# A hybrid encoder step: queries and keys turned and split out of the projection

## The chip, the cores and the metric

One NeuronCore of a Trainium2 chip runs the whole step. The metric is the device time of one execution in microseconds (us). Before the change it is 2070.28 us, the median of three runs (2068.09 to 2095.45).

## The reference, cut to what matters

A layer runs over two groups of requests that share weights: a prompt of 1024 rows and 8 sequences of 16 new rows each with a past of 256 rows. All in F32, width 1024.

```
xn = rmsnorm(x, g_attn)
aq,ak,av, bq,bk,bv, cq,ck,cv, dq,dk,dv, df = split(xn @ w_in)      # w_in: 1024 x 2820
A, 4 heads of 64: stick-breaking:  w = exp(logsig(z) - sum of softplus(z) over later keys)
B, 4 heads of 64, 2 key heads: window of 128 keys, table bias, a sink in the softmax
C, 4 heads of 2 x 32: two softmax maps (q1 k1, q2 k2) with table bias,
                      (p1 - lam * p2) @ v, rmsnorm of the head's output
D, 4 heads of 64: softmax(q k / 8 + f_q - f_k) @ v, f a running sum of log gates
h = x + concat(A,B,C,D) @ w_out
h = h + relu(rmsnorm(h) @ w_up)^2 @ w_down
h = h + sigmoid(h @ w_ple_gate) * (p @ w_ple_proj);   y = rmsnorm(h)
```

Outputs are y, and for each group its new keys and values (for B's sample the rolled window) and log gates.

## The kernel before, in words

The 1152 rows (1024 of the prompt, 128 of the sample) are nine tiles of 128 rows. The kernel is a series of blocks (projection, attention, output projection, MLP, gate and final norm), each with a barrier at its end. Matrix products use F32R, a type in which a value is split into a high part (a cast on ScalarE, ACT) and a low part (a subtraction on VectorE, DVE); `three` (L104 to L107) sums high x high, high x low and low x high. The weights come through a ring of four raw slots on the sync queue (SP), `w_load`, `w_split_hi`, `w_split_lo` (L87 to L102).

**Projection** (L196 to L443). `w_in` is cut in 6 chunks of 470 columns. For each chunk and each of the nine row tiles, TensorE (PE) runs 8 x 3 matmuls with the rows' tile stationary and 470 columns moving into one of three PSUM banks, ACT copies the bank to `proj_out`, and GpSimd (POOL) stores it to the DRAM tensor `proj_rows` (1152 x 2820), rows as rows. ACT and DVE split the next chunk's weights meanwhile. In chunk 0 the rows are also normed and turned. In the last chunk PE makes the bias table's rows and the gates' sums.

**Attention** (L473 to L1257). The order is written out by hand. A loop of two turns (`heads_loop`) runs 8 heads each, A, A, B, B, C, C, D, D (`JOBS`, even and odd), each over nine tiles: tiles 0 to 7 are 128 queries of the prompt against all earlier keys (B: at most 256), tile 8 is the sample with 272 keys of each of its 8 sequences (B: 144). All engines go through steps s. In step s PE makes the scores of tile s + 1 (`scores`, L1160), turns the weights of tile s - 1 (`turn_tile`, L1200) and multiplies those of tile s - 2 with the values (`values`, L1215). The scores are in two PSUM areas `S`, used in turn; a C tile takes both, one a map, and in the kernel before a map waits only for its own area (L1174 to L1179). DVE's step: for A a sum, a scan and a difference (`stick_breaking`, L984), for the others the row maximum (`maximum`, L998), for C also the difference of the maps (`combine`, L1034), then the head's output (`out`, L1055). ACT has the exponentials and copies turned weights out of PSUM.

A head's queries and keys are loaded by SP as rows of 64 numbers (`k_rows`, `q_rows`, `k_cache_rows`, L726 to L728, packets of 256 B), as soon as the head before has been copied. Preparing the next head is spread over tiles 1 to 5 of the present one (`AFTER`, `prep_chunks`, L584 to L595), in 9 chunks (2 of keys, 2 of queries, one mixed of sample keys and queries, 4 of cached keys; B has 2 of these). A chunk is: DVE writes each row twice side by side (`twice`, L917), PE turns four 128x128 blocks (L1139), ACT takes the high part out of PSUM (L809 to L825) and DVE the low part (`prep`, L936 to L957). So queries lie with their high part in rows 0 to 63 of the partitions and their low part in 64 to 127 (C: 32 and 32 for each map), keys stand twice, once as high parts (`k_turned_hi`) and once as low parts (`k_turned_lo`). Two matmuls (L1194; L1187 for the sample, with the queries spread over blocks of zeros) then give all four products. Their width is at least 256 columns. Masks and biases are added by a matmul of the identity with the F32 mask (L1197).

The first head of a turn of the loop is prepared before its first scores (L1076 to L1082, L1244). Values, bias tables and gates come in a second group of transfers, L731 to L747, issued when all tiles of the head before the previous one are done. DVE adds masks to the bias or the gates for the next head in step 6 of the present one (`bias` and `sample_gates`, L959 to L982, called in L1112), after `job_loaded`. POOL copies keys and values from `proj_rows` to the outputs (L759).

## Time and profile before

| | us |
|---|---|
| median of three runs | 2070.28 |
| the profiled execution | 2087.65 |
| its span, first to last instruction | 2086.0 |
| PE busy in it | 1927.6 (92%) |
| DVE busy | 938.8 (45%) |
| ACT busy | 693.5 (33%) |
| mean granted clock of PE, of full | 0.933 |

The rows come from one execution, taken by the hardware profiler. PE is TensorE's matmuls, PEld its weight loads, which overlap them. An F32 matmul is listed as two records. A record of a matmul holds its whole latency, so the spacing of starts tells what one costs in a row of them. The granted clock is given as a share of full speed (2.4 GHz). L12 is line 12 of the kernel. "<-" names what ended an idle time.

### The profile page before, as it was taken

How to read it: one execution, taken by the hardware profiler on the slowest of the kernel's cores; microseconds unless marked ns; L12 is line 12 of the kernel's file. 1: busy time of each engine (PE TensorE's matmuls, PEld its weight loads, DVE VectorE, ACT ScalarE, POOL GpSimd, SP SyncE). 2: the span in 40 equal slices, each digit the busy share in tenths (PEclk: the TensorE clock that was granted, in tenths of full speed). 3: DMA queues.
4: the chain of work that ended last, by engine and by line, in shares of the span. 5: the costliest groups of instructions: out<-in, count | busy, mean ns of one | idle time of the engine just before them, and what ended most of it. 6: DMA issues, size and time to landing. Idle time of an engine off the chain costs nothing. (4 is left out here: it accounts for less than half of the span.)

```text
span 2086.0 us, 29729 instructions
## 1 busy us (share of the span) xinstructions
PE 1927.6 (92%) x10334; PEld 1694.7 (81%) x10334; DVE 938.8 (45%) x1826; ACT 693.5 (33%) x1474; POOL 88.9 (4%) x152
## 2 busy tenths in 40 slices
PE   7999994789998679999798999999999999999898
PEld 6888883677877577778687989899998989998686
DVE  4211125877375877767345333333333333333434
ACT  5211114654254655445223222222221212211326
POOL 0111100000000000000110000000000000000000
PEclk9999996898599779989899999999999999999999
DMA  5322324344122326222431111111111111110202
GB/s 176 104 91 88 85 74 79 77 113 79 29 58 57 54 70 136 48 58 61 163 111 46 41 41 41 44 49 53 49 49 43 41 41 41 41 41 20 86 28 94
DMA packets 189252, 140.94 MB, mean 68 GB/s; under 512 B 147588, under 2 KB 157508, under 8 KB 189096
## 3 DMA queue, kind: packets, MB, share of 16 engines
q1 hardware_dynamic: 160696, 99.73, 18.7%
q0 software_dynamic: 9728, 34.63, 4.8%
q10 hardware_dynamic: 18688, 4.72, 0.9%
q8 instruction: 88, 1.44, 0.3%
q14 instruction: 52, 0.43, 0.1%
HBM read 114.95 MB, written 32.35 MB: 71 GB/s over the span
## 5 line engine op out<-in xcount | busy, mean ns | idle before, releaser
L105 PE MATMUL up<-xt_hi,w_hi_even 128*128 128x384 f32 x768 | 258.1, 336 | 1.9 <-PEq L1285 1.9
L107 PE MATMUL up<-xt_hi,w_lo_even 128*128 128x384 f32 x768 | 257.7, 336 | 0.0
L106 PE MATMUL up<-xt_lo,w_hi_even 128*128 128x384 f32 x768 | 257.6, 335 | 0.0
L107 PE MATMUL down<-w_hi_odd_b,hidden_lo 128*128 128x512 f32 x576 | 224.5, 390 | 0.0
L106 PE MATMUL down<-w_lo_odd_b,hidden_hi 128*128 128x512 f32 x576 | 224.5, 390 | 0.0
L105 PE MATMUL down<-w_hi_odd_b,hidden_hi 128*128 128x512 f32 x576 | 224.0, 389 | 0.0
L1494 DVE TENSOR_TENSOR h_rows<-down,h_rows 128x1024 f32<-128x1024 f32 x72 | 88.2, 1225 | 235.3 <-PE down L107 235.3
L1459 ACT ACTIVATE hidden_rows<-up 128x384 f32<-128x384 f32 x96 | 47.3, 492 | 415.5 <-PE up L107 415.5
L1227 PE MATMUL outs<-v_rows,probs_turned 128*128 128x64 f32 x984 | 144.0, 295 | 14.2 <-DVE probs_turned L680 11.5
L1227 PEld LDWEIGHTS outs<-v_rows,probs_turned 128*128 128x128 f32 x984 | 138.5, 216 | 19.4 <-DVE head_out L1063 7.5
L1487 DVE TENSOR_TENSOR hidden_rows<-hidden_rows 128x384 f32<-128x384 f32 x96 | 53.6, 558 | 222.8 <-ACT hidden_rows L1459 222.8
L105 PEld LDWEIGHTS up<-xt_hi,w_hi_even 128*128 128x128 f32 x768 | 144.9, 189 | 3.6 <-DVE xt_lo L132 2.1
L106 PEld LDWEIGHTS up<-xt_lo,w_hi_even 128*128 128x128 f32 x768 | 145.0, 189 | 0.8
L107 PEld LDWEIGHTS up<-xt_hi,w_lo_even 128*128 128x128 f32 x768 | 144.8, 189 | 0.0
L1212 PE MATMUL turns<-cst,probs 128*128 128x128 f32 x520 | 97.2, 311 | 35.0 <-DVE probs_turned L680 22.7
L107 PEld LDWEIGHTS down<-w_hi_odd_b,hidden_lo 128*128 128x128 f32 x576 | 108.1, 188 | 22.5
L106 PEld LDWEIGHTS down<-w_lo_odd_b,hidden_hi 128*128 128x128 f32 x576 | 108.1, 188 | 22.0
L105 PEld LDWEIGHTS down<-w_hi_odd_b,hidden_hi 128*128 128x128 f32 x576 | 108.2, 188 | 21.9
L1139 PE MATMUL turns<-cst,rows_twice 128*128 128x128 f32 x512 | 93.3, 329 | 30.8 <-DVE rows_twice L930 23.4
L680 ACT COPY probs_turned<-turns 128x512 f32<-128x512 f32 (+3 forms) x156 | 69.0, 459 | 146.9 <-PE turns L1212 146.6
L1194 PE MATMUL scores<-k_turned_hi,q_turned 128*128 128x256 f32 (+4 forms) x224 | 100.5, 449 | 14.3 <-ACT probs L856 7.5
L1212 PEld LDWEIGHTS turns<-cst,probs 128*128 128x128 f32 x520 | 74.3, 163 | 46.4 <-DVE probs_turned L680 20.7
(232 smaller groups left out, 3673.8 us busy)
## 6 DMA issues: line engine op xcount, KB each, us to landing
w_raw<-w_up SPq DMA_DIRECT2D x64, 256.0 KB, 3.0
w_raw<-w_down SPq DMA_DIRECT2D x64, 256.0 KB, 3.4
proj_rows<-proj_out POOLq DMA_DIRECT2D x54, 235.0 KB, 2.4
w_raw<-w_in SPq DMA_DIRECT2D x48, 235.0 KB, 2.7
k_rows<-proj_rows SPq DMA_DIRECT2D x16, 288.0 KB, 3.3
q_rows<-proj_rows SPq DMA_DIRECT2D x16, 288.0 KB, 4.1
v_rows<-proj_rows SPq DMA_DIRECT2D x16, 288.0 KB, 3.4
head_rows<-head_out ACTq DMA_DIRECT2D x16, 288.0 KB, 3.1
```

What stands on the lines that cost most here:

```text
L105: nc.tensor.matmul(out, xh, wh, start=first, stop=False)
L106: nc.tensor.matmul(out, xh, wl, start=False, stop=False)
L107: return nc.tensor.matmul(out, xl, wh, start=False, stop=last)
L680: copy(pt[i % 2][:, b * P:b * P + k], TB[n % 3][:, 0:k]).then_inc(q[f"read{n % 3}"], 1)
L1139: last = nc.tensor.transpose(bank[:, y * P:(y + 1) * P], tw[:, PREP[chunk] % TW, y, :], ident)
L1194: nc.tensor.matmul(dst[:, c:c + w], qt[own, e, P * t:P * (t + 1)], kt[part][own, e, k0 + c:k0 + c + w], start=part == 0, stop=False, skip_ ...
L1212: last = nc.tensor.transpose(TB[n % 3][:, (y - b) * P:(y - b + 1) * P], block_src, ident)
L1227: last = nc.tensor.matmul(dst, w[:, y * P:(y + 1) * P], vr[:, e, first_block(i) + y, :], start=y == 0, stop=y == nb - 1)
L1459: nc.scalar.activation(R[:, f % 2, :], U[f][:, 0:GT], ACT.Relu).then_inc(relu_d, 1)
L1487: nc.vector.tensor_tensor(R[:, f % 2, :], R[:, f % 2, :], R[:, f % 2, :], ALU.mult).then_inc(sq_d, 1)
L1494: nc.vector.tensor_tensor(H[:, t, :], DN[t % 2][:, :], H[:, t, :], ALU.add).then_inc(dn_add, 1)
```

## The change

It moves the turning and splitting out of attention into the projection, and changes how scores are made.

- `w_in` is taken in six blocks: 388 columns (values of A and B, gates), then the queries and keys of A, B, C and D, then 512 columns (values of C and D). Value blocks work as before and are stored as `value_rows` (1152 x 896). Queries and keys come out turned: for each of 15 pieces of 128 columns (two heads) and each group of three row tiles the weights are stationary and 384 rows moving (45 units). ACT scales queries and takes the high part, DVE the low part, POOL stores both (`q_turned_*`, `k_turned_*`).
- New keys are also kept in F32 (`kf`) and turned back by PE for the key outputs (19 turns, 56 transposes); cached keys are loaded by SP, turned for two heads at a time by PE, split by ACT and DVE, and stored (`k_cache_turned_*`, 26 turns of four transposes). PE does a turn right behind a unit's matmuls, with the two banks `TP`.
- In attention, all chunks are gone with their waits. SP loads each head in one group, at the point where values were loaded: keys, queries straight, queries crossed (low part where the high one was), cached keys, new sample keys and both kinds of spread sample queries (packets of 64 B), values, bias, gates. PE waits for the whole group before a head's first scores.
- Keys lie once, high and low part in the two halves; the second matmul uses the crossed queries. The widths are no longer raised to 256 columns.
- The two maps of a C head alternate, matmul by matmul; both wait for both score areas.
- Masks and the identity are rounded to F32R, a bias is split in two F32R parts (two more DVE instructions a head), so masks take one F32R matmul and biases two. The sample's additions stay F32.

```diff
-CW = D_IN // CHUNKS
+GT = 3 * P
+NG = TILES // 3
...
+            BLOCKS = ((388, ((512, 256), (1152, 128), (DF_COL, 4))), (512, ((0, 512),)), (384, ((768, 384),)),
+                      (512, ((1280, 512),)), (512, ((2048, 512),)), (512, ((1792, 256), (2560, 256))))
+            PIECES = {"A": (("k", 0, 256), ("q", 0, 0), ("k", 1, 384), ("q", 1, 128)),
+                      "B": (("k", 0, 256), ("q", 0, 0), ("q", 1, 128))}
+            PIECES["C"] = PIECES["D"] = PIECES["A"]
+            QK = [(1 + x, g, kind, pair, col, n) for x, g in enumerate(GROUPS) for kind, pair, col in PIECES[g] for n in range(NG)]
...
+            for m, (blk, g, kind, pair, col, n) in enumerate(QK):
+                if kind == "k":
+                    loads_here = {"A": 2, "B": 2, "C": 2, "D": 2}[g]
+                    if n < loads_here:
+                        CACHE_LOADS.append((g, loads_here * pair + n))
+                        TURNS[m] += [("c", len(CACHE_LOADS) - 1, x) for x in range(1 if g == "B" else 2)]
+                    own = (((7, 8),) if g == "B" else ((0, 1, 2, 3), (4, 5, 6, 7), (8,)))
+                    if n < len(own):
+                        TURNS[m + NG].append(("k", m // NG, own[n]))
...
+                    def qk_out(m):
+                        _, g, kind, pair, _, n = QK[m]
+                        pool.wait_ge(qk_lo, m + 1)
+                        dst = (k2 if kind == "k" else q2)[g][2 * P * pair:2 * P * pair + 2 * P, GT * n:GT * n + GT]
+                        for part, src in enumerate((stage_hi(m), stage_lo(m))):
+                            nc.gpsimd.dma_start(parts(dst, g, part), src.bitcast(F32)).then_inc(st_q[m % 2], 16)
...
+                    for m, (blk, g, kind, pair, col, n) in enumerate(QK):
+                        unit = FIRST_QK + m
+                        bank_free(unit)
+                        out = M[unit % 3][:, 0:GT].rearrange("p (t c) -> p t c", t=3)
+                        for k in range(KD):
+                            if sum(u[0] == blk for u in QK[:m]) == 0:
+                                pe.wait_ge(w_lo, blk * SLOTS + k + 1)
+                            last = three(out, WH[blk % 2][:, k, col:col + P], WL[blk % 2][:, k, col:col + P],
+                                         XH[:, 3 * n:3 * n + 3, k, :], XL[:, 3 * n:3 * n + 3, k, :], k == 0, k == KD - 1)
+                        last.then_inc(mm_full, 1)
+                        for _ in TURNS[m]:
+                            turn_bank(x)
+                            x += 1
...
                             sp.wait_ge(q["o_full"], at("o_full", TILES * (job - 1)))
-                            sp.dma_start(vr[:, e, :, :], rows_of(V_COL[g], kvh)).then_inc(done, 16)
-                            sp.dma_start(vc[:, e, 0:nb, :], cache_of(vcol)).then_inc(done, 16)
+                            sp.dma_start(kt[:, e, :].bitcast(F32), keys_[:, 0:SEQ]).then_inc(done, 16)
+                            sp.dma_start(qt[0][:, e, :].bitcast(F32), own[:, 0:SEQ]).then_inc(done, 16)
+                            for to, of in crossed:
+                                src = q2[g][bass.ds(P * h + of.start, half), :]
+                                sp.dma_start(qt[1][to, e, :].bitcast(F32), src[:, 0:SEQ]).then_inc(done, 16)
+                            n = P * cached(g)
+                            sp.dma_start(ks[:, e, :, 0:n].bitcast(F32), by_sequence(kc2[g][bass.ds(P * kvh, P), :])).then_inc(done, 16)
+                            sp.dma_start(ks[:, e, :, n:n + DEC_S].bitcast(F32), by_sequence(keys_[:, SEQ:SEQ + P])).then_inc(done, 16)
+                            sp.dma_start(spread(0, e), by_sequence(own[:, SEQ:SEQ + P])).then_inc(done, 16)
+                            for to, of in crossed:
+                                src = q2[g][bass.ds(P * h + of.start, half), :]
+                                sp.dma_start(spread(1, e)[to], by_sequence(src[:, SEQ:SEQ + P])).then_inc(done, 16)
+                            sp.dma_start(vr[:, e, :, :], vrows[:, bass.ds(V_COL[g] + HD * kvh, HD)].rearrange("(t p) d -> p t d", p=P)).then_inc(done, 16)
...
                         if t == 0:
-                            own = [WHERE[c] for c in prep_chunks(job)]
-                            for n_ in sorted({n_ % 3: n_ for n_ in sorted(own)}.values()):
-                                wait_read(pe, n_)
+                            job_loaded(pe, job)
...
-                        for m in range(2 if g == "C" else 1):
+                        maps = range(2 if g == "C" else 1)
+                        n_own = {m: (slice(HD * m, HD * m + HD) if g == "C" else slice(0, P)) for m in maps}
+                        for m in maps:
                             u = UNIT[(i, m)]
+                            if m + 1 < len(maps) and u >= 2 and group(UNITS[u - 2][0]) != "A" and group(UNITS[u - 1][0]) != "A":
+                                continue
...
-                                for c in range(0, n, 512):
-                                    w = max(min(512, n - c), 2 * P)
-                                    for part in range(2):
-                                        nc.tensor.matmul(dst[:, c:c + w], qt[own, e, P * t:P * (t + 1)], kt[part][own, e, k0 + c:k0 + c + w],
-                                                         start=part == 0, stop=False, skip_group_check=True)
...
+                            for c in range(0, n, 512):
+                                w = min(512, n - c)
+                                for part in range(2):
+                                    for m in maps:
+                                        own = n_own[m]
+                                        nc.tensor.matmul(S[UNIT[(i, m)] % 2][:, c:c + w], qt[part][own, e, P * t:P * (t + 1)],
+                                                         kt[own, e, k0 + c:k0 + c + w], start=part == 0, stop=False, skip_group_check=True)
```

## Rows read from the trace of the kernel before

**Rows 1.** Two stages: us, busy us (x instructions) of PE, PEld, DVE, ACT, POOL, PE's clock, DMA share, GB/s.

```profile
0.00:314.50 314.50, 300.30 (x1406) 260.08 (x1406) 67.45 (x117) 80.68 (x155) 29.62 (x58) 0.99 0.32 103
...
342.70:1000.00 657.30, 567.14 (x3638) 489.90 (x3638) 456.83 (x1080) 328.64 (x790) 33.38 (x46) 0.84 0.33 69
```

**Rows 2.** Timeline of PE, projection and MLP: start us, us, engine, line, operation, tiles, shape, count.

```profile
33.55 0.38 PE L107 MATMUL mm<-w_hi_even,xt_lo 128*128 128x470 f32 x1
33.76 1.04 PE L121 MATMUL tp<-cst,x_normed 128*128 128x128 f32 x8
34.55 0.46 PE L105 MATMUL mm<-w_hi_even,xt_hi 128*128 128x470 f32 x1
...
1302.49 0.33 PE L107 MATMUL up<-xt_hi,w_lo_even 128*128 128x384 f32 x1
1302.67 0.39 PE L105 MATMUL down<-w_hi_odd_b,hidden_hi 128*128 128x512 f32 x1
```

**Rows 3.** Groups by line and shape: busy us, mean ns | idle before it, releasers.

```profile
L1139 PE MATMUL turns<-cst,rows_twice 128*128 128x128 f32 x512 | 93.3, 329 | 30.8 <-DVE rows_twice L930 23.4 <-DVE q_turned L948 4.7 <-ACT probs_turned L680 1.6
...
L955 DVE TENSOR_TENSOR k_sample_turned_lo<-turns,k_sample_turned_hi 128x512 fp32r<-128x512 f32 x56 | 37.9, 688 | 7.5 <-ACT k_sample_turned_hi L824 6.7
...
L930 DVE COPY rows_twice<-k_cache_rows 128x512 f32<-128x512 f32 x56 | 23.2, 423 | 1.1 <-PE turns L1139 0.3
...
L1013 DVE TENSOR_REDUCE stats<-scores 128x1 f32<-128x1024 f32 x8 | 9.5, 1216 | 3.2 <-PE scores L1197 3.2
```

**Rows 4.** Busy time by attention head: A, A, B, B, C, and C of the second turn.

```profile
344.50:386.00 41.50, 28.28 (x169) 24.82 (x170) 36.17 (x60) 28.06 (x49) 0.00 (x0) 0.79 0.30 51
386.00:432.00 46.00, 34.68 (x223) 31.97 (x223) 36.52 (x64) 27.80 (x48) 3.42 (x6) 0.79 0.30 68
442.00:461.00 19.00, 17.99 (x144) 16.09 (x143) 15.56 (x63) 12.80 (x46) 1.61 (x3) 1.00 0.77 165
461.00:490.00 29.00, 24.86 (x163) 20.64 (x164) 21.80 (x77) 14.83 (x51) 1.62 (x3) 0.94 0.52 113
490.00:563.00 73.00, 71.20 (x300) 56.93 (x300) 35.83 (x87) 22.76 (x59) 0.45 (x1) 0.60 0.18 34
...
837.80:889.10 51.30, 48.58 (x300) 38.26 (x300) 35.69 (x89) 22.89 (x62) 0.45 (x1) 0.93 0.26 49
```

**Rows 5.** Timeline of DVE: the two D heads of turn 0, and the loop's turn.

```profile
606.82 0.35 DVE L1009 SCALAR_TENSOR_TENSOR probs<-scores,gates_of_queries,log_weights 128x128 f32<-128x128 f32 x1 [1.01 <-PE turns L1212]
...
636.34 0.43 DVE L1013 TENSOR_REDUCE stats<-scores 128x1 f32<-128x272 f32 x1
...
638.24 0.35 DVE L1009 SCALAR_TENSOR_TENSOR probs<-scores,gates_of_queries,log_weights 128x128 f32<-128x128 f32 x1 [0.23 <-PE scores L1197]
...
660.58 0.44 DVE L1013 TENSOR_REDUCE stats<-scores 128x1 f32<-128x272 f32 x1 [1.22 <-PE scores L1197]
...
676.68 0.76 DVE L930 COPY rows_twice<-k_rows 128x512 f32<-128x512 f32 x2 [4.17 <-issue]
...
689.61 0.29 DVE L990 SCALAR_TENSOR_TENSOR probs<-scores,probs 128x128 f32<-128x128 f32 x1 [1.88 <-ACT probs L836]
```

**Rows 6.** Timeline of PE in a C head: sample products, then two maps at 256 columns.

```profile
871.92 0.29 PE L1187 MATMUL scores<-k_sample_turned_lo,q_sample_spread 64*128 64x272 f32 x1
872.05 0.28 PE L1187 MATMUL scores<-k_sample_turned_hi,q_sample_spread 64*128 64x272 f32 x1
...
879.34 0.38 PE L1194 MATMUL scores<-k_turned_hi,q_turned 64*128 64x256 f32 x1
...
880.40 0.38 PE L1194 MATMUL scores<-k_turned_hi,q_turned 64*128 64x256 f32 x1
```

**Rows 7.** DMA: SP's queue in 237 to 245, in 1300 to 1400; landing of cached keys.

```profile
q1 hardware_dynamic: 4092, 1.04, 66.4%
...
q1 hardware_dynamic: 2304, 4.20, 12.6%
...
k_cache_rows<-cache_a_kv SPq DMA_DIRECT2D x4, 512.0 KB, 6.0
```

More of the change, by code:

```diff
@@ new lines, in encoder, with caches_before, turned_after_load, k_pieces @@
+            TURN_LIST = [(m, u) for m in range(len(QK)) for u in TURNS[m]]
+            TURN_AT = {u: x for x, (_, u) in enumerate(TURN_LIST)}
+            NTURN = len(TURN_LIST)
+            def caches_before(x):
+                return sum(u[0] == "c" for _, u in TURN_LIST[:x])
+            def turned_after_load(x):
+                return max(TURN_AT[u] for _, u in TURN_LIST if u[0] == "c" and u[1] == x) + 1
+            def k_pieces():
+                return [f for f in range(len(QK) // NG) if QK[f * NG][2] == "k"]
@@ L307, in _ @@
+                    for t in range(TILES):
+                        if t == 4:
+                            gates()
+                        if t == 8:
+                            act.wait_ge(l_v, 2)
+                            nc.scalar.activation(lam[:, 2:4], lam[:, 0:2], ACT.Exp).then_inc(l_a, 1)
+                        values_hi(TILES + t, FIRST_V2 + t, 512)
                 @block.vector
@@ L510, in encoder @@
             NAMES = {
-                "rows_k": "load of a head's keys", "rows_q": "of its queries", "rows_c": "of its cached keys", "job_in0": "other loads of the even head", "job_in1": "loads of the odd head",
+                "job_in0": "loads of the even head", "job_in1": "loads of the odd head",
                 "turned": "PE: a bank of transposes is full",
@@ L522, in encoder @@
                 "f_gates": "D: the sample's gates, queries less keys", "f_ready": "D: with their mask", "f_scores": "D: scores with gates",
-                "twice": "VectorE: rows of keys or queries stand twice",
-                "prep_hi": "ScalarE: the high part of turned keys or queries",
                 "c_ready": "C: weights can be transposed",
@@ L530, in encoder @@
                 "n_rstd": "C: 1 / rms", "n_scaled": "C: outputs scaled by it", "n_done": "C: the head's output is normed",
-                "bias_near": "B, C: a head's near bias with its mask", "bias_ready": "B, C: a head's bias tiles",
+                "bias_near": "B: the negated sink; C: the sample's bias", "bias_sum": "B, C: a head's near bias with its mask",
+                "bias_hi": "B, C: its high part", "bias_ready": "B, C: a head's bias tiles",
                 "stored0": "an even head's output is stored", "stored1": "an odd head's",
@@ L1098, in body @@
                                 map_factor(s - 1)
-                            if s < NT:
-                                for chunk in AFTER[s]:
-                                    twice(chunk)
                             if of_c:
@@ L1123, in _ @@
                     pe.wait_ge(primed_sem, 1)
[L1124 removed]
+                    pe.wait_ge(a_set, 4)
                     def carry_wait():
                         pe.sem_inc(pe_passed, 1)
[L1130 to L1140 removed]
                     def added(i):
@@ L1198, in scores @@
+                        for m in maps:
+                            for c, unit_, mat in added(i):
+                                last = nc.tensor.matmul(S[UNIT[(i, m)] % 2][:, c:c + mat.shape[-1]], unit_, mat, start=False, stop=True, skip_group_check=True)
                             last.then_inc(q["s_full"], 1)
```

593 lines of the change are left out of this document (319 added, 274 removed).

## The prediction

> **What bounds the kernel now.** I read the share of busy time by stage first [rows 1]. The projection (0 to 314.5 us) has PE busy 300 of 314.5 us; the attention stage (342.7 to 1000) has PE busy 567 of 657 us at a mean granted clock of 0.84 and DVE 457; the 28.2 us between them hold loads and the first head's preparation. Everything after 1000 us is not touched. Then the single matmuls, for the spacing of their starts [rows 2]; the costly groups by line [rows 3]; the attention heads one by one [rows 4]; and single instants on DVE and PE [rows 5, 6]. The reader is to see that the attention stage has no single bound. An A head is a relay of DVE and ACT (DVE busy 36.2 of 41.5 us and 36.5 of 46), a B or C head is PE (18.0 of 19, 71.2 of 73, 48.6 of 51.3) [rows 4], and one C head takes 73 us at clock 0.60 where its twin takes 51.3 at 0.93. The profiled execution took 2087.65 us (its span is 2086.0), 17 more than the median of 2070.28; that one C head holds 22 us of it. So I add up absolute lengths of heads.
>
> **The projection.** Before: 54 units of 24 matmuls with 470 columns, one each 0.213 us (33.55 to 33.76 in [rows 2]; the spacing is the same all through), 1296 x 0.213 = 276.4. After: 9 value units of 388 columns, 45 turned units of 384, 9 of 512. Starts lie 0.173 to 0.18 apart at 384 columns [rows 2]; 388 I take as 0.176 and 512, by the columns, as 0.23: 216 x 0.176 + 1080 x 0.1735 + 216 x 0.23 = 275.1. That is -1. New on PE are 45 turns (26 of cached keys with 4 transposes, 19 of new keys with 56 in all): 160 transposes. Eight took 33.76 to 34.55, 0.1 each [rows 2]; with about 0.1 per turn for the switch that is +20, all of it in the open since PE is the bound. ACT and DVE get two or three pieces of 0.5 to 0.7 us per 4.2 us unit and stay under 70%; the stores and the cached keys' buffers have two units' time to land. I charge nothing for them; if they don't land in time it is a few us (upper end 15). Sum +19.
>
> **The start of attention.** The 11 transfers of the first A head now all have to land before the first score, where transposes began after the first of five. Lost is the load (some 16 us, below) against 331 to 342.7 of preparation, and the issue waits for two memsets: 328 + 17 = 346 against 342.7, +3.5.
>
> **What leaves the attention stage.** 512 transposes on PE, 93.3 us busy; per chunk of four one copy of 0.42 and one subtraction of 0.69 on DVE, 1.1 us, and some 0.6 on ACT [rows 3]. A head prepares the next: 9 chunks, 7 where that one is B. What a chunk is worth is seen by twins.
> - D: first D head 606.82 to 638.24, with 9 chunks; second 638.24 to 660.58 to its last tile's reduction, which the first one has at 636.34 [rows 5]: 29.5 against 22.3. -7.2 a turn of the loop, -14.4.
> - A: DVE's 36.2 less 9.9, and 36.5 less 7.8, leave 26.3 and 28.7; the idle 5 to 9 us (waits for ACT) I keep. 36 a head: 2 x (41.5 + 46 - 72) = -31. Ends: 30 if ACT's waits go too, 41 if PE at its low clock takes over.
> - B: PE's 18.0 less 26 transposes at 0.113 (2.9) less the cheaper bias (next) 1.5 = 13.6; 15 a head at no wait: 2 x (19 + 29 - 30) = -36.
> - The preparation between the two turns of the loop, 676.68 to 689.61 [rows 5], falls to one score unit and a softplus: -10.
>
> **Bias and masks.** A map of C at 256 columns takes 1.06 us from start to start [rows 6], of which its two F32R products hold two steps of 0.21 and its 256-column bias in F32 the rest, 0.6, with the change of rows; without that change the bias is 0.43, nearly four times the 0.12 that an F32R product of 272 columns takes [rows 6]. Two F32R products for it are 0.24: -0.19 for some 76. It is inside the B and C numbers. Products under 256 columns in F32R (masks of 128, remainders of 128, B's sample of 144) stand nowhere in this trace: padded, they take 0.12 now. Lower end 0.11, as a transpose of 128 columns has, which changes nothing; upper end the F32 rate, 0.21 to 0.24, which costs +27 over the 136 narrow score products and the 92 narrow masks and biases. I take +3, nearest to the F32R rows.
>
> **C's score products.** Now each map is by itself: 0.8 us at the first tile, 1.06 at 256 columns [rows 6], 1.55 at 1024: some 20 us a head, and 5 for the sample (32 products 0.126 apart [rows 6], and biases). After, the maps alternate over rows 0 to 63 and 64 to 127. Lower end: two products of 512 columns in the time of one, limited by two weight loads of 0.11: 11.6 us a head. Upper end: no overlap, 14. PE's sum for a head falls from 46 to 34. But the maps now start together, only when the previous tile's second map has been exponentiated, so a new chain sets the pace: scores (1.4), two reductions (1.2 each at 1024 columns [rows 3]), the second exponential (taken as long), 0.35 of semaphores; over the eight tiles 13 + 12 + 7.5 + 2.8 = 35, and 6 for the sample. 42 us, not 34: the alternation itself is worth almost nothing here, because PE waits. 4 x 42 = 168 against 73 + 51.3 [rows 4] and the other two, 52 and 53.3 by windows of the same kind, 229.6: -61.6, of which 22 is the slow head.
> The Trainium skill, TensorE: Matmul & The Clock Gate, section Part 3, says that small matmuls on distinct row groups of the array run concurrently. By that rule alone the products of a pair take the time of one; no row here shows a pair, since the maps now follow one another.
>
> **The loads, what is late next.** All of a head's data now comes in one burst after the head before the previous one has finished, and DVE's bias or gate step waits for it in the sixth tile of the previous head; behind it on DVE stand the maxima of every later tile, then ACT, then PE. Burst of a D head: 1.5 MB in rows of 4 KB and 1 MB in rows of 1 KB at 3.0 us per MB (4.2 MB took 12.6% of 100 us [rows 7]), 7.8; 3072 packets of 64 B, at 15 ns over 16 engines 2.9 (4092 mostly tiny packets averaged 21 ns with a large load in it [rows 7]); 3200 packets of 256 B, some 5 (2048 land in 6.0 [rows 7], of which I hold some 2 for latency); gates 1.6; latency 2: 19 us. C 18, B 15. DVE comes to its wait about 4.5 tiles after the issue: in A 17 us, C 18, D 11, B 7.5. So per turn: B's second head waits 7.5, C's first 10.5, D's second 8, the rest about 0: 26, twice 52. That undoes most of what B and D gain.
> The Trainium skill, DMA: Bandwidth & Descriptors, property table, says that transfers below 512 B make the engine read, modify and write. That would make the new 64 B packets dearer than their bytes; the trace's tiny ones, at 21 ns on the average of [rows 7], don't show it.
>
> **Sum.** 19 + 3.5 - 31 - 36 - 61.6 - 14.4 - 10 + 3 + 52 = -75.5, from 2087.65: 2012 us, 2.8% under the median shown.
>
> **Rivals.**
> 1. The burst is the bound (slower): its 3072 packets of 64 B and 1024 of 1 KB, cut to short pieces for the sample, take two or three times 15 ns, or the kv copies and head stores on the same 16 engines stretch it. For: three kinds of head already reach it at 19 us. Against: the attention stage's DMA share of 0.33 [rows 1]. At 30 us the waits are 22, 22, 19, 13, 12, 11 a turn, 200 in all: 2012 + 148 = 2160. It decides from about 25 us on, where the gain against 2070 is gone. Chance 0.08.
> 2. Narrow F32R products cost four passes: 2036. For: every F32R product now is padded to 256 columns; against: no row. 0.17.
> 3. PE falls to its low level (1.2 GHz) in C and behind the waits: for, C's 0.60 and A's 0.79 [rows 4], and more waiting than before; against, fewer transposes. At half of the C time low, +34: 2046. 0.15.
> 4. The burst hides and C's maxima overlap the scores better than the chain says: stalls 10 instead of 52 and C at 38: 1955. 0.17.
> My forecast holds 0.43.
>
> **How the numbers follow.** 2% is about what a measurement of this kernel tells from no change: under 2029 is faster, over 2112 slower. Forecast mostly faster (0.36), rival 4 faster (0.17), a third of rivals 2 and 3 (0.10): 0.63. Slower: rival 1, 0.08. Same: 0.29. The range 1955 to 2080 reaches rival 4 and takes in 2 and 3 with some of the load's upper bound.
>
> **What would show it.** Right: no transposes of rows standing twice; projection about 19 us longer and still PE's; DVE's bias step waiting for a DMA, longest in B's second head and D's first; C heads of 42 us with PE idle before its scores, released by ACT's exponentials; D's heads equal but for the wait. Wrong if PE waits for banks or turned caches in the projection, if bias steps find their data there, if 128-column products start 0.21 apart, or if C is again PE's at a low clock.

## The result, and the profile after

The changed kernel takes 2265.8 us (median of 4 runs, 2254.99 to 2273.73) against 2082.86 for the kernel before in the same comparison: a ratio of 1.091, with an interval of 1.081 to 1.100. (The kernel before sometimes runs in a slower state; one of its four runs here did, and the ratio leaves it out.) The changed kernel is slower by 9%, where 2012 us had been forecast. The profiled execution took 2268.79 us, its span is 2267.2 and PE's mean granted clock 0.867.

Where the time is stands in the busy times of the two stages, the same view as [rows 1]. The columns are: stretch, us, busy us of PE, PEld, DVE, ACT and POOL, PE's clock, DMA share, GB/s.

```profile
0.00:496.00 496.00, 357.59 (x1780) 331.51 (x1781) 114.67 (x207) 103.32 (x220) 129.09 (x178) 0.85 0.54 133
525.65:1180.60 654.95, 485.75 (x3096) 439.11 (x3096) 329.56 (x800) 262.82 (x648) 33.10 (x46) 0.70 0.42 101
```

The projection had 300 busy us of PE in 314.5; now it has 358 in 496. The attention stage, from its first score to just behind its last head, had 457 busy us of DVE and 567 of PE in 657; now it has 330 and 486 in 655, so the work that was to leave did leave, and only 2 us of time went with it. SP's first load for attention gives the boundary: here the row of the kernel before, then that of the changed one.

```profile
327.71 0.42 SPq L726 DMA_DIRECT2D k_rows<-proj_rows  x1
```

```profile
508.08 0.38 SPq L917 DMA_DIRECT2D k_turned<-k_turned_A  x1
```

It comes 180.4 us later. The profiled executions differ by 181, so that is all of the loss; the forecast for this stage was 19.

The waits of 80 to 470 us in the changed kernel say who stands there (who waited for whom: us in total, times, longest):

```profile
DVE x_rows L510 <- ACT x_rows L443: 137.1, 18, 18.8
PEld tp L638 <- DVE k_cache_parts L497: 77.0, 12, 14.4
PE tp L638 <- ACT x_normed L448: 65.6, 7, 14.2
ACT x_rows L443 <- DMA k_turned_A<-x_rows: 36.7, 3, 19.6
ACT k_cache_parts L435 <- DMA k_cache_turned_D<-k_cache_parts: 36.5, 4, 17.0
ACT x_rows L443 <- DMA k_turned_D<-x_rows: 35.9, 2, 18.2
ACT k_cache_parts L435 <- DMA k_cache_turned_A<-k_cache_parts: 32.7, 4, 14.7
```

Read it from below. ACT waits, up to 19.6 us at a time, for stores of an earlier part to land, because the part's buffer is the one that it writes next. DVE waits for ACT, PE's turns wait for DVE's and ACT's copies, and PE's next columns stand behind the turn on PE. The DMA view of the same stretch (KB of one transfer, median us to landing) gives the stores' price:

```profile
DMA packets 65593, 50.62 MB, mean 130 GB/s; under 512 B 45834, under 2 KB 55229, under 8 KB 65578
q0 software_dynamic: 53375, 36.45, 44.8%
k_cache_turned_C<-k_cache_parts POOLq DMA_DIRECT2D x16, 256.0 KB, 10.7
k_cache_turned_A<-k_cache_parts POOLq DMA_DIRECT2D x14, 256.0 KB, 12.6
q_turned_A<-x_rows POOLq DMA_DIRECT2D x12, 192.0 KB, 8.8
```

The engines are not full on the average (share 0.54 above) and yet 256 KB take 10.7 to 12.6 us to land. GpSimd's own timeline shows that it also stops without a releaser (13.47 us ahead of one issue):

```profile
99.91 1.59 POOL L361 DMA_DIRECT2D k_turned_A<-x_rows  x2
101.49 0.81 POOL L361 DMA_DIRECT2D q_turned_A<-x_rows  x1
115.77 0.80 POOL L361 DMA_DIRECT2D q_turned_A<-x_rows  x1 [13.47 <-issue]
```

In the attention stage I measure a head from one sample output to the next: ACT's copy of the turned sample output, one a head. In the kernel before the 16 copies stretch over 604.2 us (394.6 to 998.8), in the changed one over 607.6 (571.8 to 1179.4). The intervals, in us, each named by the head that ends it (the first A head has none):

| | A | B | B | C | C | D | D | A | A | B | B | C | C | D | D |
|---|---|---|---|---|---|---|---|---|---|---|---|---|---|---|---|
| before | 46.8 | 19.0 | 28.5 | 73.5 | 51.8 | 32.0 | 25.3 | 71.4 | 46.8 | 19.0 | 28.5 | 51.3 | 53.3 | 32.0 | 25.2 |
| after | 47.2 | 31.7 | 40.6 | 47.1 | 45.2 | 43.0 | 25.9 | 51.2 | 38.4 | 32.6 | 39.9 | 47.6 | 47.8 | 44.0 | 25.4 |

C gives back 42 us in all and the loop's turn 20; each B head loses 12 and the first D head of a turn 11 to 12. A B head in the changed kernel, by the rows of three engines: the copy that ends the A head before, SP's first and last group of the next load, DVE's bias step that waits for the load, and the copy that ends the B head.

```profile
619.07 0.26 ACT L1075 COPY out_turned<-outs 64x128 f32<-64x128 f32 x1 [7.59 <-PE outs L1354]
```

```profile
619.84 0.35 SPq L917 DMA_DIRECT2D k_turned<-k_turned_B  x1
623.50 4.84 SPq L925 DMA_DIRECT2D q_sample_spread_straight<-q_turned_B  x1
638.34 0.36 SPq L939 DMA_DIRECT2D head_scalar<-swa_sinks  x1
```

```profile
640.88 0.15 DVE L1114 TENSOR_SCALAR head_scalar_negated<-head_scalar 128x1 f32<-128x1 f32 x1 [13.67 <-DMA head_scalar<-swa_sinks]
```

```profile
650.74 0.26 ACT L1075 COPY out_turned<-outs 64x128 f32<-64x128 f32 x1 [1.87 <-PE outs L1354]
```

Of the 31.7 us, 21 pass from SP's first issue until DVE can go on (18.9 of them in the issues, one after another), and 10 more for the last three tiles. The whole B head is a load and its tail.

### The profile page after: what moved, and what is told of

Read it like the earlier page. It is cut to its first block and busy times, and to the rows that moved or that the text cites. A ratio compares the mean times of both kernels' runs of the same rounds, so it can differ in the third digit from the quotient of the medians.

```text
span 2267.2 us, 28303 instructions
## 1 busy us (share of the span) xinstructions
PE 1896.3 (84%) x10134; PEld 1710.8 (75%) x10134; DVE 851.6 (38%) x1619; ACT 645.1 (28%) x1387; POOL 188.0 (8%) x272
## 5 line engine op out<-in xcount | busy, mean ns | idle before, releaser
L1346 PE MATMUL outs<-v_rows,probs_turned 128*128 128x64 f32 x984 | 166.1, 325 | 112.2 <-DVE head_out L1208 84.1
L1346 PEld LDWEIGHTS outs<-v_rows,probs_turned 128*128 128x128 f32 x984 | 159.0, 244 | 124.8 <-DVE head_out L1208 62.1
L1314 PE MATMUL scores<-k_turned,q_turned_straight 128*128 128x512 f32 (+5 forms) x224 | 89.9, 519 | 69.5 <-ACT probs L1038 31.1
L113 PEld LDWEIGHTS up<-xt_hi,w_lo_even 128*128 128x128 f32 x768 | 144.8, 189 | 0.0
L1333 PE MATMUL turns<-cst,probs 128*128 128x128 f32 x520 | 105.7, 333 | 1.7 <-ACT probs L1024 1.7
L1314 PEld LDWEIGHTS scores<-k_turned,q_turned_straight 128*128 128x128 f32 (+1 forms) x224 | 45.9, 260 | 80.8 <-issue 35.8
L1155 DVE TENSOR_REDUCE stats<-scores 128x1 f32<-128x272 f32 (+8 forms) x76 | 51.5, 705 | 79.0 <-PE scores L1318 78.5
## 6 DMA issues: line engine op xcount, KB each, us to landing
k_cache_turned_A<-k_cache_parts POOLq DMA_DIRECT2D x16, 256.0 KB, 12.6
```

Of the source, the lines that this page charges most:

```text
L113: return nc.tensor.matmul(out, xl, wh, start=False, stop=last)
L1155: nc.vector.tensor_reduce(st_[:, col:col + 1], src[:, 0:n], AX.X, ALU.max, negate=True).then_inc(q["m_ready"], 1)
L1314: nc.tensor.matmul(S[UNIT[(i, m)] % 2][:, c:c + w], qt[part][own, e, P * t:P * (t + 1)], kt[own, e, k0 + c:k0 + c + w], start=part == 0, s ...
L1333: last = nc.tensor.transpose(TB[n % 3][:, (y - b) * P:(y - b + 1) * P], block_src, ident)
L1346: last = nc.tensor.matmul(dst, w[:, y * P:(y + 1) * P], vr[:, e, first_block(i) + y, :], start=y == 0, stop=y == nb - 1)
```

## The experiments

All start from the changed kernel. "Attention begins" is SP's first load for it (508.08 in the changed kernel); "attention" is the stretch of the 16 copies (607.6 there).

**1. Where a store's rows go.** In the changed kernel each store of a high or low part goes to rows of a group of 64 (C: 32), a gap, and the next group.

```diff
-                return dst.rearrange("(x u d) c -> u x d c", u=2, d=HALF[g])[part]
+                return dst[P * part:P * part + P, :]
```

> Edit of the changed kernel: each store of a high or low part goes to one block of 128 neighbouring rows in DRAM, where it went to two (C: four) groups of rows with gaps between; bytes, queue, waits and loads are as they were. A head then loads rows that mix parts of two heads, so the scores differ from the reference. Theory 1, the pattern: the traced stores come with 268 (192 KB) to 375 (256 KB) packets of 8 or 12 bytes each, which the value stores with plain rows don't have, and POOL stands up to 13.5 us idle with no releaser; without them landing falls from 8 to 13 us to some 3, and the loads of attention begin at 350 to 370 us instead of 508: about 2110 in all. Theory 2, the bytes (31 MB more are written in the projection): landing stays above 8 us and the time stays at 2266. Theory 3, the software queue with any pattern: packets of 8 and 12 bytes stay, and so does the time.

Measured: 2106.61 us, attention begins at 351.20. Of the 180.4 us, 156.9 are gone, with the same bytes, queue, buffers and waits. The DMA view of 80 to 340 us:

```profile
DMA packets 25840, 51.75 MB, mean 199 GB/s; under 512 B 5288, under 2 KB 14657, under 8 KB 25823
q0 software_dynamic: 11770, 37.34, 39.2%
k_cache_turned_C<-k_cache_parts POOLq DMA_DIRECT2D x16, 256.0 KB, 4.4
k_cache_turned_A<-k_cache_parts POOLq DMA_DIRECT2D x13, 256.0 KB, 5.2
q_turned_A<-x_rows POOLq DMA_DIRECT2D x12, 192.0 KB, 2.3
```

Landing falls from 10.7 and 12.6 to 4.4 and 5.2, and the packets under 512 B from 45834 to 5288; in the packet records some 41800 packets of 8 or 12 bytes on GpSimd's queue are gone. GpSimd's queue moves 37.34 MB with 39.2% of 16 engines over 260 us, where the changed kernel needs 44.8% over 390 us for 36.45 MB: there the same bytes cost some 1.7 times the engine time. PE is busy 254.67 of these 260 us at a clock of 1.00. Theory 1 holds; the bytes (theory 2) and the queue by itself (theory 3) don't.

**2. Another queue, same rows; and another queue, plain rows.** The stores of turned parts are issued by ACT, one unit later; then the same with the rows of experiment 1.

```diff
-                                nc.gpsimd.dma_start(parts(dst, g, part), chl[:, n, part, :].bitcast(F32)).then_inc(st_c[n], 16)
+                                nc.scalar.dma_start(parts(dst, g, part), chl[:, n, part, :].bitcast(F32)).then_inc(st_c[n], 16)
...
+                        if m:
+                            xs = stores_of(m - 1, xs)
                         act.wait_ge(mm_full, FIRST_QK + m + 1)
```

> Edit: the stores of turned and split parts and of the turned-back keys are issued by ACT, one unit later than the unit they belong to, where POOL issued them; pattern and bytes are the same. Theory 1 (pattern, whichever queue): no gain, and ACT is held by the issues on top: 2266 or more. Theory 3 (what POOL's queue does for this pattern): landing falls to 3 to 4 us, attention begins at 350 to 380: about 2110 to 2130. Theory 2 (bytes): 2266.

> Edit: the plain rows of e1_flat with the stores issued by ACT as in e2_act; the scores differ from the reference as there. If in e2_act the pattern kept each store on two of the 16 DMA engines (51 GB/s and 2 of 16 engines busy there), plain rows put them on all 16: landing 2 to 3 us, ACT's issues fall from 4.7 us to some 0.5, and attention begins near 350 as in e1_flat, 2100 to 2115. If ACT's queue is slow for another reason (its issues wait in order behind DVE's parts), attention stays late, above 2200.

Measured: 2484.4 us with the rows apart, where attention begins at 731.07; 2099.42 us with plain rows (one run), where it begins at 347.16. With the rows apart ACT's queue is 219 us worse than GpSimd's; theory 1 had "2266 or more". This run shows best what the pattern does, because nothing else is under way: a stretch with C's stores alone, and one with D's.

```profile
461.00:469.00 8.00, 8.00 (x48) 7.93 (x47) 1.16 (x2) 0.49 (x1) 0.00 (x0) 0.96 0.26 101
500.00:508.00 8.00, 0.00 (x0) 0.00 (x0) 0.56 (x1) 0.86 (x2) 0.00 (x0) 0.50 0.13 51
```

D's destination has two groups of rows: DMA share 0.13, two of the 16 engines, 51 GB/s. C's has four: share 0.26, four engines, 101 GB/s. The Trainium skill, DMA: Bandwidth & Descriptors, section Why a DMA increments its semaphore by 16 and not by 1, states this rule: the engines of a transfer are the largest number up to 16 that divides the slowest dimension of both sides. By that rule a destination of 2 x 64 rows gets two engines, 4 x 32 four and 128 sixteen; these rows agree on the two and the four. ACT is held by its issues too, 4.7 us each (18.68 for four), where with plain rows two take 0.97:

```profile
110.17 18.68 ACTq L422 DMA_DIRECT2D k_cache_turned_A<-k_cache_parts  x4
```

```profile
132.81 0.97 ACTq L422 DMA_DIRECT2D k_cache_turned_B<-k_cache_parts  x2
```

When GpSimd issues the stores, they overlap. GpSimd's queue in two stretches of the changed kernel, first 104 to 113 us with five to six stores under way, then 120 to 122 us, where packets of one store of `q_turned_A` alone move (packets, MB, share of 16 engines):

```profile
q0 software_dynamic: 1030, 1.10, 56.1%
q0 software_dynamic: 27, 0.09, 11.3%
```

The single store has 11.3%, under two of 16 engines, as on ACT's queue. Five to six together have 56.1%, nine engines, so they are not all on the same two. On ACT's queue they are: the D stretch above stays at 0.13 though four stores of 256 KB are issued from 486.54 to 506.38. That fits its 219 us. What no run parts for GpSimd's queue is how much of the loss is the few engines of a store, how much the small packets, and how much its stops.

**3. Deeper buffers.** Four staging buffers instead of two, three for the cached keys' parts instead of two.

```diff
-CR = 2
+CR = 3
...
-                        if m >= 2:
-                            act.wait_ge(st_q[m % 2], 32 * (m // 2))
+                        if m >= 4:
+                            act.wait_ge(st_q[m % 4], 32 * (m // 4))
```

> Edit: the turned parts have four staging buffers instead of two and the cached keys' parts three instead of two, in memory that stands free in this stage; stores as they were. If only latency was short (12 us against two units of 4.2), four units' time (17 us) hides it and attention begins near 350 to 370: about 2115. If POOL's queue itself takes in fewer stores than are made (some 3.5 us for each, 152 stores in 390 us), depth buys little: attention begins after 480, time above 2235.

Measured: 2215.06 us, attention begins at 455.09. That is 53 us gained and 104 short of experiment 1: between the two cases forecast, nearer to the one in which the rate is short. The stores' landing is no shorter (17.7 us for k_cache_turned_A, 13.3 for C). Deeper buffers hid a part of the late stores; they didn't make up for a queue that took stores in more slowly than they were made.

**4. The same places, more stores.** Each store is cut into two (C: four) of neighbouring rows; nothing moves in DRAM.

```diff
-                            nc.gpsimd.dma_start(parts(dst, g, part), src.bitcast(F32)).then_inc(st_q[m % 2], 16)
+                            for x_ in range(P // HALF[g]):
+                                own = slice(HALF[g] * x_, HALF[g] * x_ + HALF[g])
+                                nc.gpsimd.dma_start(dst[HALF[g] * (2 * x_ + part):HALF[g] * (2 * x_ + part + 1), :],
+                                                    src[own, :].bitcast(F32)).then_inc(st_q[m % 2], 16)
```

> Edit of the changed kernel: every store keeps its place in DRAM, but one store with two (C: four) groups of rows becomes two (four) stores, each of one block of 64 (32) neighbouring rows; queue, bytes, buffers and loads are as they were. If the trouble is the gap between groups of rows inside one transfer, landing falls to 2 to 5 us though the rows lie where they did; GpSimd now issues 364 stores at 0.7 to 0.8 us, some 280 us, over the stage's 345, so the stage may be some 10 us longer than in e1_flat: about 2110 to 2120. If it is where the rows lie, nothing changes: 2266.

Measured: 2140.31 us, attention begins at 377.96, landing 2.0 to 3.9 us. So it is the gap inside one transfer, not where the rows lie. The stage is 27 us longer than in experiment 1, more than the 10 I gave GpSimd's issues (it is busy 192.87 of 260 us against 87.90).

**5. The maps of C one after another.** Undoes the alternation alone: each map waits for its own area, then its products, its bias, its signal.

```diff
-                                for part in range(2):
-                                    for m in maps:
+                        for m in maps:
+                            pe.wait_ge(q["e_ready"], unit_at("e_ready", *UNITS[u - 2]))
...
+                                    for part in range(2):
```

> Edit of the changed kernel: a C head's maps follow one another again, each with its own wait for its score area, products, bias and signal; nothing else. Theory A, the alternation is worth almost nothing because both maps start only when the later area is read: the C intervals stay within 3 us of 47.1 and 45.2 (first turn) and 47.6 and 47.8 (second), total 2255 to 2275. Theory B, pairs of products on the two halves of the rows take the time of one: without them PE has 10 us more in each C head, and C heads get 4 to 10 us longer, about 2290. Theory C, starting each map on its own area is worth more than the pair: C heads 3 to 6 us shorter, about 2250.

Measured: 2335.9 us (2328.45 to 2351.36), 70 above the changed kernel. In its profile attention is 58 us longer. The C intervals are 62.0, 58.1, 62.0 and 58.1, so the alternation is worth 10 to 15 us a head, 52 in all: theory B and more. First the two C heads of the changed kernel, then of this one:

```profile
691.30:738.40 47.10, 37.48 (x266) 33.03 (x266) 25.79 (x67) 18.60 (x50) 0.45 (x1) 0.76 0.41 89
738.40:783.60 45.20, 36.22 (x252) 32.33 (x251) 24.68 (x61) 18.37 (x48) 4.79 (x5) 0.74 0.43 104
```

```profile
693.10:755.10 62.00, 59.08 (x266) 48.80 (x266) 26.59 (x67) 18.68 (x50) 0.44 (x1) 0.61 0.29 68
755.10:813.20 58.10, 55.00 (x251) 46.03 (x251) 25.38 (x61) 18.45 (x49) 4.78 (x5) 0.59 0.33 81
```

With the maps in turn PE is busy 59 of 62 us at a mean clock of 0.61, near its low level; with pairs 37 of 47 at 0.76. What of the 15 us is the overlap and what is the clock, this run doesn't part. The pairs themselves stand in PE's timeline of the changed kernel, at 1024 columns:

```profile
716.22 0.50 PE L1314 MATMUL scores<-k_turned,q_turned_straight 64*128 64x512 f32 x2 [1.60 <-ACT probs L1038]
716.55 0.40 PE L1314 MATMUL scores<-k_turned,q_turned_crossed 64*128 64x512 f32 x2
716.78 0.41 PE L1314 MATMUL scores<-k_turned,q_turned_straight 64*128 64x512 f32 x2
717.02 0.40 PE L1314 MATMUL scores<-k_turned,q_turned_crossed 64*128 64x512 f32 x2
```

Each row holds the products of both maps, and the rows are 0.23 to 0.24 apart. One product of 512 columns alone stands 0.23 ahead of its successor in this kernel (573.94 to 574.17, in an A head): two products in the time of one.

**6. What the burst of loads costs.** Five variants. In the first the bias, sink or gate loads come first and have a semaphore of their own, so that DVE waits for them alone. In the second the sample's queries and new keys come with their rows' other columns, and GpSimd spreads them in SBUF, in place of 4096 packets of 64 B a head.

```diff
+                            sp.dma_start(bi[:, e, :], src[:, 0:2 * P]).then_inc(first, 16)
...
-                        job_loaded(dve, job)
+                        near_loaded(dve, job)
```

> Edit, attention alone: bias, sink or gates of the next head are loaded first and counted on a semaphore of their own, and DVE's bias or gate step waits for them alone; the wait for all loads stands only before PE's first score of the head. Theory A, DVE's early wait is what the burst costs: 74 us of DVE's idle time end with these loads; 50 to 74 of it go, the B heads fall from 32 and 41 us to some 18 and 24: about 2200. Theory B, the burst itself is late for the head's first score: the wait moves to PE, and only 10 to 25 us go: about 2245.

```diff
-                            sp.dma_start(spread(0, e), by_sequence(own[:, SEQ:SEQ + P])).then_inc(done, 16)
...
+                        for dst, src in ((qz[0][:, e, :], qt[0]), (qz[1][:, e, :], qt[1]), (None, kt)):
...
+                            nc.gpsimd.tensor_tensor(dst, src, one[:, :].unsqueeze(2).broadcast_to((P, DEC_B, DEC_S)), ALU.mult).then_inc(q["spread"], 1)
```

> Edit, attention alone: the sample's queries and new keys come with their 1024 other columns in rows of 4.6 KB, and GpSimd, idle in this stage, spreads them by sequence in SBUF (3 small multiplications by one for each head); the 4096 packets of 64 B a head and their issues (some 8 us on SP) are gone. Theory A, the burst (21 us from the first issue to the last landing) is what the attention stage pays: it falls to some 12 us, B intervals fall by 8 each and the first D's by 6, the start by 6: 50 us in all, about 2215. Theory B, the burst's time is that of its large rows: 5 to 10 us, about 2258.

Measured: 2264.4 us for the order of the loads (2254.31 to 2268.15; no difference that can be told, and less than theory B had, though attention is 11 us shorter in its profile), 2240.64 for the spreading (2227.27 to 2245.49), between its two theories. With the loads in another order most of DVE's wait is gone (10 us of 85 are left) and PE's first scores have it instead:

```profile
PE scores L1324 <- DMA v_cache_rows<-cache_c_kv: 33.7, 2, 17.3
PE scores L1324 <- DMA v_cache_rows<-cache_b_kv: 20.9, 2, 10.6
PE scores L1324 <- DMA log_weights<-fcum_prompt: 16.6, 2, 8.4
```

With the spreading attention is 576.8 us, 31 shorter: B heads 28.2 to 36.9, the first D heads 39.5 and 33.2. Both point at the burst's length: its order alone gave nothing, and a shorter one gave time.

The third variant puts experiment 1's rows in a usable form (the loads of a head take its parts in pieces of 64 or, for C, 32 rows) with the spreading on GpSimd. The fourth adds to it a second queue: bias, sink and gate loads go on GpSimd's, beside the rest on SP's. A fifth is the control: the same order and the same semaphores, all on SP.

```diff
+                            for to, at_, _ in pieces:
+                                sp.dma_start(kt[to, e, :].bitcast(F32), k2[g][bass.ds(k_at + at_, half), :]).then_inc(done, 16)
...
+                            if job + 2 < len(JOBS):
+                                near_loads(j, job + 2)
```

> Edit: stores as in e1_flat (plain blocks of 128 rows), loads of a head in pieces of 64 rows (C: 32), so that every row comes to its place and the scores are the reference's; and the spreading on GpSimd of e8_spread. From e1_flat's 2106.6 the piecewise loads cost some 3 us of issue a head where loads are late and the spreading gives back what e8_spread gives: with theory A of e8_spread about 2070, with theory B about 2105.

> Edit: e9_layout, and the next head's bias, sink or gate loads are issued by GpSimd's queue beside the others on SP's, counted apart, with DVE's bias or gate step waiting for them alone. Theory A, the length of the burst (some 21 us from a head's end to the last landing, most of it issued one transfer after another on one queue) is what the attention stage pays: with the two shares side by side it falls to some 13 us, B intervals go from 30 and 40 to some 23 and 31, the first D's from 40 to 32; attention is some 45 us shorter than in e9_layout and the kernel about 2065, at or below the kernel before. Theory B, it is the 16 engines' time and not the issue: at most 10 us go, about 2098.

> Edit: e9_layout with the same loads still on SP, but first in the burst and counted apart. The burst keeps its length; only its order changes. Theory A: the wait moves from DVE to PE's first score and a few us go (some 10 in all, as e5_near showed on the changed kernel): about 2098. If instead order is what counts, it does as well as e10_near.

Measured: 2107.95 us for the third (theory B's number), 2070.22 for the fourth (12 runs, 2063.02 to 2079.60), 2111.99 for the control. The fourth has the lowest time of the study; its ratio to the kernel before, run beside it, is 0.995 (0.991 to 0.998), which by a bar of 2% is the same time. Two queues, and not the order, are what helps: attention is 588.9 us in the third, 603.5 in the control and 572.4 in the fourth, with B intervals of 25.5, 34.4, 25.3 and 34.7, first D heads of 31.6 and 34.3. Both forecasts for attention missed. The control was to gain a few us and lost 15. The fourth was to gain 45 and gained 17: its B and D heads gave back 35 us, but its A and C heads got 18 us longer, at lower granted clocks (the first interval 43.0 us at 0.68 where the third has 38.4 at 0.78, the first C head 51.4 at 0.62 where the third has 49.7 at 0.71). DVE's waits for loads in it:

```profile
DVE bias_sample L1144 <- DMA head_scalar<-rel_bias: 14.6, 2, 7.5
DVE head_scalar_negated L1141 <- DMA head_scalar<-swa_sinks: 12.0, 2, 7.1
```

That is 27 us where the changed kernel has 64 in these two places; PE's first scores wait 17 us in return.

**7. Whole loads.** Experiment 4's stores keep the rows in place, so the loads can stay whole; then the high parts' stores go to ACT's queue, to see if GpSimd's issues hold the projection.

```diff
+                        if m:
+                            high_out(m - 1)
...
+                            nc.scalar.dma_start(dst[2 * HALF[g] * x_:2 * HALF[g] * x_ + HALF[g], :], src[own, :].bitcast(F32)).then_inc(done, 16)
```

> Edit: the stores of e12_pieces with the attention stage of e10_near, whose loads can now stay whole (3 or 5 transfers where e10_near has 6 or 12). If the length of a head's burst still counts, it is shorter by some 2 us (C: 5) than in e10_near and attention by some 10 to 15 us; with a projection as in e1_flat that makes 2055 to 2065, with GpSimd late in the projection 2070 or more.

> Edit: e13_pieces_near, with the high parts' stores issued by ACT, one unit later, and the low parts' by GpSimd as before, each with semaphores of its own; places in DRAM, pieces and bytes are the same. If e12's and e13's projection is 27 us longer than e1_flat's because GpSimd issues 364 stores at some 0.75 us (busy 191 of 240 us there), half of them is 140 us and attention begins near 352 instead of 378: about 2055, below the kernel before. If it is the number of transfers in flight or ACT's issues (182 at some 0.5 us, up to 8 in a 4.2 us unit of C) that hold the stage, it stays near 2080 or goes up.

Measured: 2080.25 us and 2080.44, ratios of 1.002 (0.999 to 1.005) and 0.999 (0.995 to 1.003). Neither differs from the kernel before. Attention is the shortest of all, 556.4 and 553.2 (B heads 23.0 to 31.2), but it begins at 376.38 and 378.55, where 352 was the hope for the second. Halving GpSimd's issues (busy 101.55 of 240 us in the second, 191.42 in the first) changes nothing. ACT's issues may have taken their place; ahead of C's columns ACT is held 5.79 us by eight of them:

```profile
214.01 5.79 ACTq L456 DMA_DIRECT2D k_cache_turned_C<-k_cache_parts  x8
219.93 0.48 ACT L483 COPY x_normed<-mm 128x384 f32<-128x384 f32 x1 [6.66 <-issue]
```

Whether those 27 us are the issues or the transfers behind them stays open. A version with plain rows for the stores and whole loads would need another order of C's rows; it wasn't tried.

## Why the prediction was wrong

- **The projection, the step that failed.** I wrote: "the stores and the cached keys' buffers have two units' time to land. I charge nothing for them; if they don't land in time it is a few us (upper end 15)." It was 157 us. Bytes were counted and the form of the destination wasn't: a transfer whose outer dimension is 2 or 4 uses that many engines. By an estimate from the 51 GB/s, a unit of A makes two stores of 3.9 us and, with a cached block, two to four of 5.1, against 4.2 us for the unit. The stores ran partly side by side and the queue still fell behind, and the two-deep buffers then made unit after unit wait. That the form of the destination is the cause is shown (experiments 1 and 4); what in GpSimd's queue makes it so dear is open. The rows that I had are of plain stores (235 KB of `proj_rows` land in 2.4 us in the kernel before) and said nothing of this form, so the upper end of 15 had no source.
- **The rest of the projection held.** In experiment 1, without that fault, attention begins 23.5 us later than before; 19 were forecast for turns and columns (in that sum 1296 x 0.213 is 276.0 and not 276.4, which changes nothing). PE is busy at a clock of 1.00 all through.
- **What leaves the attention stage left.** No transposes of rows standing twice, DVE's busy time down by 127 us, PE's by 81. But heads are not the sum of their engines' work.
- **The loads.** The mechanism was right, the place too (DVE's bias step in B's heads and D's first), the size was not. The burst of B was 21 us where I had 15, C's 23.9 (651.4 to 675.4) for 18. The term of 52 for stalls measured 85: 13.7 and 14.4 for the sink, 18.9 and 16.1 for C's bias, 10.4 and 11.5 for D's gates (the 74 in the first expectation of experiment 6 is too low). And what follows the wait had been taken as already paid: 10 us after it in B's first head, 16 in B's second (640.9 to 650.7, 675.4 to 691.3), where 15 a head without a wait left 7. The B intervals sum to 144.8 where the forecast has 95: that is 50 of the 95 us by which attention was missed. D's are 22 over, C's 19, A's 7. Attention was to give back 98 us and gave 2. My rival 1 (the burst is bound) thus was truer for attention than my forecast, and it got 0.08.
- **C.** The forecast of 42 a head was 5 short (45.2 to 47.8). The chain that was to set the pace is there: in C heads PE waits 28 us in all for ACT's exponentials before its scores. "The alternation itself is worth almost nothing here, because PE waits" is false: experiment 5 puts 10 to 15 us on it. I compared two sums at full clock; PE in turn does not run at full clock. The rule of the Trainium skill, TensorE: Matmul & The Clock Gate, section Part 3, that small products on distinct row groups run concurrently, is borne out by the pairs above.
- **A.** The later A intervals are 47.2, 51.2 and 38.4 for a forecast of 36 a head and the turn of the loop: with the first head 7 over, and the one at 47.2 holds 9 that the one at 38.4 has not (see the clock below).
- **Narrow F32R products.** Rival 2 falls. From PE's timeline of the first A head in the changed kernel, a product of 128 columns and its mask in F32R, then a product of 256 columns and a mask of 128, each with its successor:

```profile
562.17 0.27 PE L1314 MATMUL scores<-k_turned,q_turned_crossed 128*128 128x128 f32 x1
562.28 0.28 PE L1318 MATMUL scores<-masks_rounded,ident_rounded 128*128 128x128 f32 x1
562.39 0.29 PE L1333 MATMUL turns<-cst,probs 128*128 128x128 f32 x1
565.53 0.28 PE L1314 MATMUL scores<-k_turned,q_turned_crossed 128*128 128x256 f32 x1
565.65 0.22 PE L1318 MATMUL scores<-masks_rounded,ident_rounded 128*128 128x128 f32 x1
565.71 0.40 PE L1333 MATMUL turns<-cst,probs 128*128 128x128 f32 x2
```

The first mask and its product take 0.11, my lower end; the second mask takes 0.06, half of what 256 columns take and below that end. None takes the 0.21 of the upper end. Padding to 256 columns bought nothing.

- **The clock.** Rival 3 was at work: the attention stage's mean clock is 0.70 where it was 0.84. It named C; the traces show it best in A. Two A heads of the changed kernel, with the same 199 matmuls:

```profile
571.85:619.07 47.22, 38.52 (x199) 35.49 (x199) 28.79 (x48) 22.34 (x37) 1.61 (x3) 0.63 0.35 84
903.71:942.12 38.41, 30.84 (x199) 27.38 (x199) 28.49 (x48) 22.24 (x37) 1.61 (x3) 0.78 0.44 103
```

DVE and ACT do the same work in both, and the one at clock 0.63 is 9 us longer, no faster than the 46.8 of the kernel before. In the five other runs whose attention stage is the changed kernel's (experiments 1 to 4), these two heads take 38.5 to 39.7 us at 0.70 to 0.78, 43.0 at 0.68 and 47.0 at 0.63, so a difference of up to 9 us in one A head between two profiles can't be put down to their edits.

## What to carry to other kernels

Before moving a tensor into a layout in DRAM, write down the access pattern of each transfer, side by side, and look at its slowest dimension: here a store with 2 or 4 there ran on 2 or 4 of 16 engines (51 and 101 GB/s), and splitting it (experiment 4, 130 us earlier) or moving the gap into the load's side (157) was worth more than deeper buffers (53). Where a head's (tile's, expert's) data can only be fetched once a buffer is free, the time from first issue to last landing was part of every head shorter than it; share the issues between two queues and take out transfers that only rearrange small pieces. And when work is taken from a relay of engines, ask what its clock and its loads do at the lower load before counting the difference.

## What was not expected of the hardware

- A store to 2 x 64 rows ran at 51 GB/s and a DMA share of 0.13, to 4 x 32 rows at 101 and 0.26; with 128 neighbouring rows 256 KB landed in 4.4 us in a stage that moved 199 GB/s.
- On GpSimd's queue such stores also came with some 41800 packets of 8 or 12 bytes (some 10 ns each), which neither plain rows nor ACT's queue show; what they are isn't known.
- An issue on ACT's queue held ACT for 4.7 us a store where two engines carry it, for 0.5 with plain rows.
- The same A head took 38.4 us at a mean granted clock of 0.78 and 47.2 at 0.63, in one execution.
- Two F32R products of 512 columns on rows 0 to 63 and 64 to 127 start within the same row of the timeline and take 0.23 us together.
